# A decoder step with eight window caches: the samples' softmax divided behind the values, and the first keys in other buffers

## The reference

```python
# per sample b, token t, head h; three branches (window, dilation): (128,1), (512,4), (2048,16)
logits = einsum('bthd,btjhd->bhtj', q, kg) + bias        # j: the picked cache rows of a branch
lse = logsumexp(logits, -1); p = exp(logits - lse)
o = einsum('bhtj,btjhd->bthd', p, vg)                    # merged over the branches by softmax(lse)
x = x + concat(o, pool_mix(u)) @ w_out
x = x + cross_attn(rmsnorm(x), mk, mv) ; x = x + moe(rmsnorm(x))   # top 4 of 32 experts
# outputs besides y: the eight key and value windows, each moved on by 4 rows
```

## Time and profile before

| what | value |
|---|---|
| runs | 1402.57, 1412.00, 1412.21 us; median 1412.00 us |
| profiled execution | 1408.78 us, span 1406.9 us, mean granted TensorE clock 0.965 |
| PE, DVE, ACT, POOL busy | 1260.8, 479.9, 232.0, 68.1 us |
| last sample's loop turn ends (`values(6)`) | 252.03 us |
| `out` group 0 starts | 255.24 us |
| `out` group 2 ends | 291.6 us |
| expert stream | from about 465 us to the end |

### The profile page before, as it was taken

One profiled execution on the slowest core, in us unless ns is written; L12 is line 12 of the kernel. 1 busy time (PEld: TensorE's weight loads), 2 busy tenths in 40 slices (PEclk: granted clock), 3 DMA queues, 4 the chain that ended last, 5 costly groups with the idle time before them and its releaser, 6 DMA issues.

```text
span 1406.9 us, 16526 instructions
## 1 busy us (share of the span) xinstructions
PE 1260.8 (90%) x6407; PEld 530.5 (38%) x6407; DVE 479.9 (34%) x1033; ACT 232.0 (16%) x448; POOL 68.1 (5%) x69
## 2 busy tenths in 40 slices
PE   7988987988897999998999989999899999999986
PEld 5443333456644333332333323333333333333332
DVE  2367889332326412212232122321223212232124
ACT  1334343212311100110101100110011010011102
POOL 2000000005007000000000000000000000000000
PEclk9998988999997999999999999999999999999999
DMA  9999799999989899999999999999999999999993
GB/s 349 344 356 418 295 376 345 359 380 341 345 356 370 344 430 426 429 426 428 428 429 428 429 428 429 428 428 429 429 428 429 428 429 428 429 428 429 428 429 154
DMA packets 51740, 557.14 MB, mean 396 GB/s; under 512 B 7021, under 2 KB 9301, under 8 KB 15885
## 3 DMA queue, kind: packets, MB, share of 16 engines
q1 hardware_dynamic: 50629, 553.04, 96.1%
q0 software_dynamic: 1072, 3.57, 0.6%
HBM read 552.02 MB, written 71.72 MB: 443 GB/s over the span
## 4 chain that ended last, share of the span: by engine, by line
DMA 52%; PE 38%; DVE 7%; SPq 1%; issue 1%; ACT 1%; DVEq 0%; ACTq 0%; PEldq 0%
DMA wide<-in_w_gate_up 49%; PE bank L1926 12%; PE bank L1619 3%; PE bank L1639 3%; PE bank L1955 2%; PE bank L1721 2%; PE bank L1661 2%; PE bank L1484 2%; DMA wide<-in_cache_k_win 1%; PE bank L1552 1%; PE bank L1480 1%; DVE small L1153 1%; DMA slim<-in_w_xq 1%; PE bank L1709 1%; DVE wide L1150 1%
## 5 line engine op out<-in xcount | busy, mean ns | idle before, releaser
L1926 PE MATMUL bank<-wide,att 128*64 128x512 f32 x2048 | 463.3, 596 | 59.0 <-DMA wide<-in_w_gate_up 58.7
L1926 PEld LDWEIGHTS bank<-wide,att 128*64 128x64 f32 x2048 | 139.4, 136 | 362.9 <-issue 228.6
L1955 PE MATMUL bank<-slim,att 128*64 128x512 f32 x1024 | 226.8, 595 | 0.0
L1394 DVE TENSOR_SCALAR att<-bank 128x512 f32<-128x512 f32 x32 | 22.1, 692 | 469.6 <-PE bank L1926 469.6
L1955 PEld LDWEIGHTS bank<-slim,att 128*64 128x64 f32 x1024 | 70.6, 137 | 152.2 <-issue 149.2
L1373 DVE TENSOR_TENSOR x<-x,bank 128x512 f32<-128x512 f32 x68 | 46.6, 685 | 233.2 <-PE bank L1908 226.5
L962 ACT ACTIVATE att<-att 128x512 f32<-128x512 f32 x32 | 20.2, 632 | 518.0 <-DVE att L1394 518.0
L1908 PE MATMUL bank<-tb,att 128*128 128x512 f32 (+1 forms) x192 | 84.7, 611 | 1.8 <-ACT tb L971 1.3
L971 ACT ACTIVATE tb<-bank 64x512 f32<-64x512 f32 x64 | 37.9, 593 | 234.0 <-PE bank L1955 233.7
L1639 PE MATMUL bank<-slim,ta 128*128 128x512 f32 x128 | 60.6, 629 | 3.1 <-DVE wide L1151 3.1
L1153 DVE TENSOR_REDUCE small<-wide 128x24 f32<-128x1536 f32 x28 | 49.1, 1753 | 1.0
(11 more groups left out here) (289 smaller groups left out, 1153.7 us busy)
## 6 DMA issues: line engine op xcount, KB each, us to landing
wide<-in_w_gate_up SPq DMA_DIRECT2D x128, 2048.0 KB, 25.4
slim<-in_w_down SPq DMA_DIRECT2D x64, 2048.0 KB, 22.0
out_k_win_sample<-in_cache_k_win SPq DMA_DIRECT2D x16, 2044.0 KB, 20.4
out_v_win_sample<-in_cache_v_win SPq DMA_DIRECT2D x16, 2044.0 KB, 28.1
wide<-in_w_in SPq DMA_DIRECT2D x8, 1024.0 KB, 15.9
wide<-in_cache_v_win SPq DMA_DIRECT2D x8, 1024.0 KB, 5.5
wide<-in_cache_mem_k SPq DMA_DIRECT2D x8, 1024.0 KB, 23.9
wide<-in_cache_mem_v SPq DMA_DIRECT2D x8, 1024.0 KB, 14.3
```

The costliest lines, as they stand in the source:

```text
L1926: ins = M(bk[half[h], :], rows[:, k, :], wide[:, k, c:c + 512], start=False, stop=k == KC - 1)
L1955: ins = M(bank_y[half[h], :], aT[:, f % 4, f // 4, :], slim[:, f, 512 * h:512 * h + 512], start=f == 0, stop=f == KC - 1)
```

## The change

**The samples' softmax.** The exponentials go to `values` undivided. In the same function PE adds them up with a column of ones: 16 matmuls of one column each, into column b of an eighth bank. DVE takes the reciprocal of that column (128 x 1, `part_of_sum`), and ACT copies the product with it as the scale (`keep`, now on ACT). The mask goes: `turn_values` picks each head's block by itself, with 8 matmuls of 64 rows in place of 4 of 128. `sums`, `shares` and POOL's addition are gone, and `values` waits for `sexp` and the reciprocal of the sample before.

**The prompt's softmax.** DVE makes only the reciprocal (`unit_sum`); ACT multiplies (`unit_share`, two instructions a unit) and then goes on to `keep`, `unit_pt`, `sample_exp`, `late_values`, `sample_out`.

**The first keys.** The window of sample 0 lies in `tb` and `mkT` and no longer in `slim`, so six of the eight pieces of `w_xk` are issued ahead of the loop's windows. The key windows 1 and 2 change buffers, and window 2 is issued with window 1. COPIES has two copies fewer ahead, two more next to it, and one more in each of turns 2 and 5. The four pool products come later on PE and ACT; the first two rows of sample 1 earlier on PE and DVE.

```diff
-        COPIES = [7, 1, 1, 1, 1, 2, 1, 2, 2, 2, 3, 2, 1, 3]
+        COPIES = [5, 1, 3, 1, 2, 2, 2, 2, 2, 2, 3, 2, 1, 3]
...
             load(sp, "toep", bias, skew)
+            slim_first(range(6))
             copy(COPIES.pop(0))
+            sp.wait_ge(w_read, 3)
+            window(kwin[1], i["cache_k_win"], 1, k_in[1])
             sp.wait_ge(w_read, 5)
-            window(kwin[1], i["cache_k_win"], 1, k_in[1])
+            window(kwin[0], i["cache_k_win"], 2, k_in[0])
             sp.wait_ge(w_read, 7)
             window(vwin, i["cache_v_win"], 0, v_in)
-            sp.wait_ge(stored["pool"], 48)
             sp.wait_ge(scored, 1)
-            slim_round(0)
+            slim_first(range(6, KC))
             copy(COPIES.pop(0))
             for b in range(1, DEC_B):
-                if b + 1 < DEC_B:
+                if 1 < b < DEC_B - 1:
                     sp.wait_ge(scored, b)
                     window(kwin[(b + 1) % 2], i["cache_k_win"], b + 1, k_in[(b + 1) % 2])
...
+            def unit_share(u):
+                nk = P * (UNITS[u][1] + 1)
+                act.wait_ge(rsum, u + 1)
+                for h in range(2):
+                    c = 10 + 4 * (u % 2) + h
+                    ins = A(lg[u % 2][:, h, 0:nk], lg[u % 2][:, h, 0:nk], ACT.Copy, scale=stat[:, c:c + 1])
+                ins.then_inc(scaled, 1)
+
+            def keep(b):
+                if b:
+                    b_, use = place(("pvt", b - 1))
+                    act.wait_ge(bank_full[b_], use + 1)
+                act.wait_ge(rz_in, b + 1)
+                ps, s = product(act, "pv", b)
+                A(kept, ps[:, :], ACT.Copy, scale=rz[:, b:b + 1]).then_inc(s, 1)
...
             for b in range(1, DEC_B):
+                unit_share(b - 1)
+                if b >= 2:
+                    keep(b - 2)
                 unit_pt(b - 1)
+                sample_exp(b - 1)
+                late_values(b - 1)
                 if b >= 2:
                     sample_out(b - 2)
-                sample_exp(b - 1)
-                late_values(b - 1)
...
+            unit_share(DEC_B - 1)
+            keep(DEC_B - 2)
             unit_pt(DEC_B - 1)
+            sample_exp(DEC_B - 1)
+            late_values(DEC_B - 1)
             sample_out(DEC_B - 2)
             unit_out(DEC_B - 1)
-            late_values(DEC_B - 1)
-            sample_exp(DEC_B - 1)
...
-            def sums(b):
-            def shares(b):
-            def keep(b):
+            def part_of_sum(b):
+                b_, use = place(("pv", b))
+                dve.wait_ge(bank_full[b_], use + 1)
+                V.reciprocal(rz[:, b:b + 1], sx_bank[:, b:b + 1]).then_inc(rz_in, 1)
+
+            def unit_sum(u):
+                c = 10 + 4 * (u % 2)
+                dve.wait_ge(expd, 2 * u + 2)
+                V.reciprocal(stat[:, c:c + 2], stat[:, c:c + 2]).then_inc(rsum, 1)
...
             def values(b):
-                pe.wait_ge(prob, b + 1)
+                pe.wait_ge(sexp, b + 1)
+                pe.wait_ge(rz_in, b)
                 pe.wait_ge(v_in, 64 * (b + 1))
                 pe.wait_ge(late_v, b + 1)
                 ps, s = take(pe, "pv", b)
...
+                for kind in range(4):
+                    for t in range(DEC_T):
+                        n = NS if kind == 3 else P
+                        M(sx_bank[32 * t:32 * t + 32, b:b + 1], flat[0:n, kind, :], ones[0:n, 0:1], start=kind == 0, stop=kind == 3,
+                          tile_position=(0, 32 * t))
...
-                for c in range(4):
-                    ins = M(ps[:, 4 * c:4 * c + 4], kept[:, P * c:P * c + P], own[:, AW:AW + DEC_T], start=True, stop=True)
+                for h in range(HEADS):
+                    ins = M(ps[64 * (h % 2):64 * (h % 2) + 64, 4 * (h // 2):4 * (h // 2) + 4], kept[:, HD * h:HD * h + HD],
+                            own[:, DEC_T * h:DEC_T * h + DEC_T], start=True, stop=True)
```

More of the change, by code:

```diff
@@ L293, in build @@
                 add(*f)
+        for g in range(4):
+            add("pool", g)
         for b in range(1, DEC_B):
@@ L493, in copy, with slim_first @@
                     sp.dma_start(dst, src).then_inc(stored["copies"], 16)
+            def slim_first(ks):
+                for k in ks:
+                    sp.dma_start(slim[:, k, :], wch("w_xk")[k]).then_inc(slim_in[k], 16)
             def slim_round(r):
@@ L512, in _ @@
             sp.wait_ge(cleared, 1)
-            window(kfirst, i["cache_k_win"], 0, k_in[0])
+            src = i["cache_k_win"][0, 0]
+            sp.dma_start(near_first, src[PAST - 512:PAST].rearrange("(p t) h d -> p t (h d)", p=P)).then_inc(k_in[0], 16)
+            far = src.rearrange("(p t) h d -> p t (h d)", p=P)[0:96, 0:4, :].rearrange("(g r) t n -> r g t n", r=3)
+            for r in range(3):
+                sp.dma_start(far_first[r:P:4], far[r]).then_inc(k_in[0], 16)
             b, use = place(("tr1", 2, 1))
@@ L769, in _, with late_rows @@
             A(uS[:, :, :, 0:STATE], ps[:, 0:480].rearrange("p (g b n) -> p g b n", g=4, n=STATE), ACT.Copy).then_inc(s, 1)
-            def late_rows(win, done):
+            def late_rows(late, win, done):
                 for s in range(4):
-                    ins = A(win[32 * s:32 * s + 32, 8, :], win[96:128, s, :], ACT.Copy)
+                    ins = A(late[32 * s:32 * s + 32, :], win[96:128, s, :], ACT.Copy)
                 ins.then_inc(done, 1)
@@ L803, in _ @@
             turned_in(2), turned_in(0)
[L804 to L807, removed]
+            late_keys(1)
             rows_out(1)
@@ L881, in _ @@
                 if t == 1:
+                    keep(DEC_B - 1)
                     sample_out(DEC_B - 1)
@@ L1175, in _ @@
             dve.wait_ge(loaded["toep"], 16)
-            for g in range(4):
-                b_, use = place(("pool", g))
-                dve.wait_ge(bank_full[b_], use + 1)
+            dve.wait_ge(stored["pool"], 48)
+            dve.wait_ge(k_in[1], 64)
+            dve.wait_ge(late_k, 2)
+            row(1, 0), shift(0)
             logits(0)
             for b in range(1, DEC_B):
-                dve.wait_ge(expd, 2 * b)
-                share(b - 1, b, P * (UNITS[b - 1][1] + 1))
+                if b > 1:
+                    unit_sum(b - 1)
                 dve.wait_ge(k_in[b % 2], 64 * (b // 2 + 1))
                 dve.wait_ge(late_k, b + 1)
-                for t in range(DEC_T):
+                for t in range(0 if b > 1 else 1, DEC_T):
                     row(b, t)
-                    if t < 3:
-                        (shift, sums, shares)[t](b - 1)
-                    if b >= 2 and t == 0:
-                        keep(b - 2)
+                    if b == 1 and t == 1:
+                        unit_sum(0)
+                    if b > 1 and t == 0:
+                        shift(b - 1)
+                        part_of_sum(b - 2)
                     if t == 2:
@@ L1193, in _ @@
                 largest_score(b)
-            dve.wait_ge(expd, 2 * DEC_B)
-            share(DEC_B - 1, DEC_B, P * (UNITS[DEC_B - 1][1] + 1))
-            shift(DEC_B - 1), keep(DEC_B - 2), sums(DEC_B - 1), shares(DEC_B - 1)
+            unit_sum(DEC_B - 1)
+            shift(DEC_B - 1), part_of_sum(DEC_B - 2)
             for u in range(2):
@@ L1224, in _ @@
                 if t == 0:
-                    keep(DEC_B - 1)
+                    part_of_sum(DEC_B - 1)
                 norm(5 + t, n, x[0:n, t, :], hn[0:n, t, :], 6 + t)
@@ L1535, in _ @@
             turn_rows(0)
-            pe.wait_ge(loaded["wpool"], 16)
-            for g in range(4):
-                pe.wait_ge(pooled, g + 1)
-                ps, s = take(pe, "pool", g)
-                M(ps[:, 0:T], wpool[:, g, :], dT[:, g, :], start=True, stop=True).then_inc(s, 1)
             def row(b, t):
@@ L1559, in _ @@
                     row(0, t)
+            row(1, 0), row(1, 1)
             turn_rows(1)
@@ L1675, in _ @@
                     fill(f)
+            pe.wait_ge(loaded["wpool"], 16)
+            for g in range(4):
+                pe.wait_ge(pooled, g + 1)
+                ps, s = take(pe, "pool", g)
+                M(ps[:, 0:T], wpool[:, g, :], dT[:, g, :], start=True, stop=True).then_inc(s, 1)
             for b in range(1, DEC_B):
```

87 lines of the change are left out of this document (42 added, 45 removed).

## The result

The changed kernel takes 1414.57 us in the median (1411.77 to 1420.83, 20 runs) against 1410.97 us before (1402.57 to 1415.25, 20 runs). The ratio is 1.0031, with a 95% interval of 1.0018 to 1.0045: +4.4 us, between +2.5 and +6.3. The forecast was 1420 us, +9.6 by its sum. The time lies in the range and the sign is right; the size is somewhat under half of what I forecast.

A forecast was written before the change was run, and what follows sets the result against it. In the loop DVE and PE were taken as nearly full, joined by the softmax, with transfers limiting any gain; 1.5 + 7.2 + 1.3 + 0.3 - 0.7 = +9.6 us, forecast 1420 us, range 1405 to 1434.

The forecast's parts named there:

- The tail: Behind the loop, `out` 0 waits for sample 7's late value rows, starting 10.4 us after the last turn, not 3.2: +7.2 us.
- Sums: Sample 7's sums stand between `out` 0 and `out` 1 on PE; 32 one-column passes at 0.042 us each: +1.3 us.
- `turn_values`: On PE, 16 passes for 8; sample 7's stands ahead of `out` 2: +0.3 us.
- The loop: The loop ends 1.5 us later than now, between 2 us earlier and 6 later.
- PE works 1.6 us more a turn: In the loop, PE's added sums and `turn_values` make its turn 18.5 to 19.1 us of work plus some 1.4 waiting.
- The transfer bound: In the loop, transfer engines idle only 13.3 us and two added copies take 10 to 12.1: end at most 1 to 3 earlier.
- Behind `out` 2: After `out` 2, PE's 0.72 us wait for `w_xq` goes (-0.7 us); otherwise a chain with few gaps takes up little.
- The experts: Two copies fewer ahead of the second expert's weights gain 0 to -1 us, taken as 0, since SP's issues wait for PE.
- The slower one: PE's sums cost 3.8 us each and the lower clock stays: up to +26.6 us, 1438; beyond +14, with a late-loop case, 0.26.
- The faster one: PE's clock stays at the upper level, shortening loop turns to about 17.5 us: -10 us, 1402; chance 0.08 beyond -14.
- The tail that does not wait: Behind the loop, the last window comes sooner, 7.2 shrinks to 3 or less: +3 to +5, 1414; chance with no effect 0.10.

The follow-up runs named there:

- e5: Kernel before with only the two softmax changes, ACT's old order behind the loop: 1402.57 us, ratio 0.9952 to before.
- e1: Changed kernel with ACT's old order behind the loop, `unit_out(7)` ahead of sample 7's late value rows: 1405.45 us, ratio 0.9976 to before.
- e9: e5 with ACT's division of the prompt's unit put ahead of the copy of the fill's bank: ratio 0.9956 to before.
- e12: e5 with the changed kernel's order of ACT behind the loop: ratio 1.0025 to before, 10.3 us above e5.
- e2: Kernel before with only ACT's new order behind the loop, sample 7's late value rows ahead of `unit_out(7)`: ratio 1.0058 to before, +8.2 us.
- e3: Changed kernel with one copy fewer in each of turns 2 and 5: ratio 1.0014 to before.
- e4: Changed kernel with both ACT's old order behind the loop and the two copies fewer in it: ratio 0.9958 to before.
- e6: Kernel before with only the first keys, early `w_xk`, new copy list and moved steps; old softmax and ACT order: ratio 0.9986 to before.
- e8: e7 with two more copies moved to between cross attention and the experts, one from ahead of the loop, one from turn 5: ratio 0.9969 to before.
- e7: e4 with ACT's division of the prompt's unit put ahead of the copy of the fill's bank: ratio 0.9956 to before.

## Why the prediction was half right

- **The tail (+7.2): right, a little small.** Four pairs of kernels that differ in ACT's order alone give 8.2, 7.8, 7.9 and 10.3 us. The chain was the one I named: single buffer, window, late rows, two small copies. `out` 0 came 11.4 and not 10.4 us after the loop, since the window took 8.4 us from issue to ACT's start, not 7.3. What I did not foresee is a stretch at the lower clock level after PE's idle time, 2 us of `out` 0 here: from `out` 0's start to `out` 2's end the five traces with the wait take 1.6 to 3.1 us more than the same kernel's 36.3 or 36.6 us without; of the nine without, only the second one of before shows such a stretch (1.2 us).
- **Sums (+1.3) and `turn_values` (+0.3): too high.** The 32 passes of one column take 0.54 us (0.71 at the lower clock), 0.017 each, not L1820's 0.042 with 32 columns. That it is the columns is not shown, since the two rows differ in more: L1820's passes all write the same 32 output rows, the sums' passes four times 32 rows (`tile_position` in the diff). Passes of 512 columns show what this can be worth: 2.78 / 24 = 0.116 us where `values` writes four times 32 rows, 14.00 / 32 = 0.44 us where `out` 0 writes all 128 at once. By the rule that I cited of the Trainium skill (page "TensorEngine Tiling (Array Packing)", section "Instruction Overhead"), 0.8 us were estimated; the row is below that, and decides. `turn_values` with 64 rows became shorter, 0.64 for 0.95.
- **The loop (+1.5): the step that failed.** The step was "PE works 1.6 us more a turn", and with it a turn of 20 us, "no shorter than now unless the clock stays up"; the clock's rise I put into a rival of 8%. PE did not work more. From the end of `values(0)` to that of `values(6)`, six turns in which my term makes 9.6 us, it was busy for 109.28 us before, 106.79 in the changed kernel and 105.21 in e5:

```profile
125.00:252.03 127.03, 109.28 (x487) 45.19 (x487) 112.91 (x169) 49.72 (x107) 6.81 (x14) 0.85 0.89 347
124.94:251.44 126.50, 106.79 (x728) 44.89 (x727) 100.23 (x145) 55.57 (x124) 4.14 (x9) 0.92 1.00 387
123.04:246.53 123.49, 105.21 (x728) 45.16 (x727) 100.47 (x145) 57.67 (x127) 4.16 (x9) 0.93 0.92 360
```

  In the mean of three traces each it is 108.8 us in the old loop, 107.0 in the changed one (e1's included) and 104.6 with the softmax alone (e5, e9, e12). The granted clock rose with the new softmax: 0.88 to 0.93 in the loops of the ten traces that have it, 0.83 to 0.87 in the four that don't, and in the changed kernel the values and fills alone became 8.6 us shorter. I had argued for a rise from PE's busy share, but that share did not grow in these turns (0.86 before, 0.84 in the changed kernel). The softmax alone ends the loop at 246.5, 5.6 us before the mean of three traces of the old one (252.1, from 250.5 to 253.9; e2's is one of them). The transfer bound (at most 1 to 3 us earlier with two copies more) held: three traces of the changed loop (e1's included) end at 250.9 in the mean, 1.2 before that same mean, which is less than the old loop scatters. Without the two copies it ends at 246.0 and 247.2 (e3, e4): what the turns won, the copies took up.
- **Behind `out` 2 (nothing but -0.7): put too low.** I gave it nothing because PE's order there is a chain with few gaps. In the mean of two traces of each kernel `out` 2 ends 9.7 us later than before, near the 10.3 that my terms give up to there, since the loop and the sums came out lower and the tail higher; then the stretch is 5.2 us shorter, which leaves 4.5. How much of that the change causes is open, as said above.
- **All but the tail**, then: forecast +2.4, timed -3.4 (e1, -5.4 to -1.3). Of these 5.8 us e1's trace has some 4.9 before the end of `out` 2 (289.8 for 291.5, where my terms give +3.1), in the loop and the sums above all. With the tail's +7.8 that is the measured +4.4. By the experiments it is -6.8 for the softmax, +3.4 for the early part with its copies on top of it (2.5 of them the two copies in the loop), +7.8 for the tail's order. The parts do not simply add: the early part alone, e6, is -2.0 and not +3.4.
- **The experts (0): right here, but not for my reason alone.** The transfer engines stand idle from 460 to 470 us in the changed kernel; in e8, which moves copies towards them, they hold the stream up.
- **The rivals.** The slower one fell with the sums' price. Its sum was wrong besides: with the sums at 2 us, 5 + 7.2 + 2 + 0.3 - 0.7 is +14 and not +12, so it would have decided from 2 us on and not from 2.3. The faster one named the clock, which did rise, but had the tail and the transfers against it; without both it is nearest to e5, the fastest version with e7 and e9, 0.5% below before. The tail that does not wait has the measured number, 1414, by luck alone: PE did stand still, for 8.96 us.

Why the clock rises is not shown. PE waits in e5's loop some 25 us, as before, but in other places (14.4 us ahead of `turned`, 10.5 ahead of the sums); no run separates the place of a wait from its length. Nor is the clock shown to be all of what the softmax wins: e9's loop has 0.88, hardly more than the 0.87 of the second trace of before, and ends 4.1 us earlier. DVE's lighter turns and the wait for the shares that went have a part that no run separates.

## What to carry to other kernels

An order written by hand for a loop may be wrong at its end: in the turns the late value rows stood where the next values needed them, behind the last turn they put the next stage behind a transfer that nobody there needed. Where transfers are nearly full beside the engines, price every engine's gain by the transfers first, and every moved transfer by the place where it lands, since it costs nothing only as long as that place has room. A bound that is worked out from rows says how far a stage can move, not that it will move there: ask besides whether each engine's work in a turn grows or shrinks, which here I had wrong for PE.

## What the hardware showed that I had not expected

Matmul passes with one output column, sent to four places of 32 output rows, took 0.017 us each at the upper clock level, against 0.042 for passes of 32 columns that all went to one place. After 7 to 10 us in which PE had nothing to do, the product behind it began at the lower clock level (0.50) in all five traces, so that the idle stretch cost 1.6 to 3.1 us more than its length. The second trace of before shows such a beginning without an idle stretch, so that the wait is not its only cause.
